# Second block's mixers: all differences of the first row block ahead of the last taps, and the convolution's transposes one quarter unit later

## What is computed

```python
def diff_attention(q, k, v, lam, slopes):
    ...
        s = s - slopes[None, :, None, None, None] * dist
        p = jax.nn.softmax(s, axis=-1)
        a = p[:, :, 0] - lam * p[:, :, 1]
        return jnp.einsum("bhqk,bkhe->bqhe", a.astype(v.dtype), v)

def conformer_conv(u, w_dw, b_dw, ln_g, ln_b):
    a, gate = jnp.split(u, 2, axis=-1)
    z = a * jax.nn.sigmoid(gate)
    z = lax.conv_general_dilated(...) + b_dw        # 31 taps, 256 channels, one filter each
    return jax.nn.silu(layer_norm(z, ln_g, ln_b))

y = jnp.concatenate([y_conv, y_pool, y_attn], axis=-1) @ w_out[l]
```

## Time and profile before

| what | us |
|---|---|
| median of three runs | 2058.48 |
| the profiled execution, whole | 2058.67 |
| its span from the first to the last instruction | 2056.8 |
| TensorE busy in the span | 2043.0 |
| VectorE busy | 1501.4 |
| ScalarE busy | 1094.8 |
| GpSimd busy | 128.9 |

### The profile page before, as it was taken

How to read it: one execution, slowest core, us unless ns; L and a number is a source line. 1 busy time by engine, 2 the same in 40 slices (tenths; PEclk the granted TensorE clock), 3 DMA queues, 4 the chain that set the end, 5 groups by cost and what they waited for, 6 DMA issues and landing times.

```text
span 2056.8 us, 27845 instructions
## 1 busy us (share of the span) xinstructions
PE 2043.0 (99%) x10803; PEld 1743.8 (85%) x10803; DVE 1501.4 (73%) x2262; ACT 1094.8 (53%) x1640; POOL 128.9 (6%) x140
## 2 busy tenths in 40 slices
PE   9999999999999999999999999999999999999998
PEld 8888888888888888888888888878888888878887
DVE  7776677777677767777766777798667777798766
ACT  5444665544554456655446455675445545675443
POOL 1000100000000001000001000160000000160000
PEclk9999999999999999999999999999999999999999
DMA  8655545555555555455555756426555656425553
GB/s 255 201 188 163 195 152 199 185 184 193 191 186 184 194 166 174 167 191 191 187 193 189 240 185 225 154 97 201 191 193 189 205 185 217 161 94 195 194 191 127
DMA packets 105540, 378.82 MB, mean 184 GB/s; under 512 B 12174, under 2 KB 12838, under 8 KB 105153
## 3 DMA queue, kind: packets, MB, share of 16 engines
q1 hardware_dynamic: 102224, 368.16, 54.5%
q0 software_dynamic: 2208, 7.71, 1.2%
q10 hardware_dynamic: 976, 1.17, 0.2%
HBM read 375.73 MB, written 1.27 MB: 183 GB/s over the span
## 4 chain that ended last, share of the span: by engine, by line
PE 95%; DVE 3%; DMA 1%; issue 0%; ACT 0%; SPq 0%; POOLq 0%; POOL 0%; DVEq 0%; ACTq 0%
PE pb L515 30%; PE pb L523 16%; PE pb L414 14%; PE pb L415 14%; PE pb L419 14%; DMA raw<-in_W 1%; PE pb L575 1%; PE pb L442 1%; PE pb L462 1%; PE pb L464 1%; PE pb L463 1%; DVE scr L1821 1%; DVE wlo L1806 1%; DVE scr L2500 0%; PE pb L639 0%
## 5 line engine op out<-in xcount | busy, mean ns | idle before, releaser
L1806 DVE TENSOR_TENSOR wlo<-raw,whi 128x1024 fp32r<-128x1024 f32 (+1 forms) x680 | 822.8, 1218 | 52.4 <-ACT whi L1177 52.2
L1177 ACT ACTIVATE whi<-raw 128x1024 fp32r<-128x1024 f32 (+1 forms) x684 | 707.1, 1045 | 279.1 <-PE pb L523 156.0
L515 PE MATMUL pb<-XT,whi 128*128 128x512 f32 x2784 | 695.2, 391 | 1.3 <-DVE XT L1821 0.7
L515 PEld LDWEIGHTS pb<-XT,whi 128*128 128x128 f32 x2784 | 509.8, 188 | 100.1 <-ACT whi L1177 1.4
L523 PEld LDWEIGHTS pb<-XT,wlo 128*128 128x128 f32 x2784 | 379.7, 190 | 27.1
L523 PE MATMUL pb<-XT,wlo 128*128 128x256 f32 x2784 | 388.2, 282 | 0.0
L1931 DVE TENSOR_REDUCE sbuf_s<-pb 128x256 f32<-128x512 f32 x240 | 154.6, 686 | 230.6 <-PE pb L523 230.6
L414 PE MATMUL pb<-whi,HTh 128*128 128x512 f32 x796 | 313.6, 394 | 0.7 <-DVE HTl L1950 0.4
L415 PE MATMUL pb<-whi,HTl 128*128 128x512 f32 x796 | 311.6, 391 | 0.0
L419 PE MATMUL pb<-wlo,HTh 128*128 128x512 f32 x796 | 302.0, 389 | 0.0
L1248 ACT ACTIVATE sbuf_s<-sbuf_s 128x256 f32<-128x256 f32 x120 | 49.6, 419 | 340.2 <-DVE sbuf_s L1938 340.1
(11 more groups left out here) (267 smaller groups left out, 1663.5 us busy)
## 6 DMA issues: line engine op xcount, KB each, us to landing
raw<-in_W SPq DMA_DIRECT2D x694, 512.0 KB, 4.3
raw<-in_W SPq DMA_DIRECT2D x8, 264.0 KB, 2.8
scr<-in_bc POOLq DMA_DIRECT2D x2, 640.0 KB, 5.3
raw<-in_W SPq DMA_DIRECT2D x4, 256.0 KB, 6.2
scr<-scratch POOLq DMA_DIRECT2D x8, 128.0 KB, 4.5
scr<-mrow POOLq DMA_DIRECT2D x2, 512.0 KB, 5.2
scr<-in_slope POOLq DMA_DIRECT2D x1, 1024.0 KB, 11.2
scr<-in_Pg POOLq DMA_DIRECT2D x1, 1024.0 KB, 14.4
```

The source lines that it names most:

```text
L515: pe.matmul(pb[b + j][:, :], h[:, k:k + P], xs, start=c == 0, stop=False)
L1177: return act.activation(o, i, ACT.Copy, scale=scale)
L1806: dve.tensor_tensor(low_w(u)[:, 0:c], raw[u % RAW_SLOTS][:, 0:c], high_w(u)[:, 0:c].bitcast(F32), ALU.subtract).then_inc(*up("lo", u))
```

## The change

On TensorE the transposes of the convolution, `turn_conv(4)`, go from ahead of the quarter `out(18, 2)` to behind it. On VectorE the four differences of row block 0 go ahead of the taps 26 to 30 and stand in a row; the taps follow, with `pool_low(0, 7)` after tap 28. The three small steps of the weights of row block 1 stand in a row, two of its differences come ahead of the statistics, and the other two between `conv_stats` and `conv_mean`. ScalarE, GpSimd and SyncE keep their order, and no instruction is added or taken away.

```diff
@@ tensor: mixer2 @@
                 out(18, 1)
                 turn_maps(0, 2, 6)
                 turn_maps(0, 0, 5)
+                out(18, 2)
                 turn_conv(4)
-                out(18, 2)
                 values(0, 7)
                 turn_maps(1, 2, 6)
                 turn_maps(1, 0, 5)
@@ vector: mixer2 @@
                 pool_low(1, 7)
+                difference(0, 3)
+                difference(0, 2)
+                difference(0, 1)
+                difference(0, 0)
                 tap(26)
-                difference(0, 1)
                 tap(27)
-                difference(0, 3)
                 tap(28)
+                pool_low(0, 7)
                 tap(29)
-                difference(0, 2)
-                difference(0, 0)
+                tap(30)
                 weights_inv(1)
-                tap(30)
                 weights_ratio(1)
-                pool_low(0, 7)
                 weights_lam(1)
+                difference(1, 2)
+                difference(1, 3)
                 conv_stats(0, 4)
                 conv_stats(1, 4)
+                difference(1, 1)
+                difference(1, 0)
                 conv_mean(0)
                 conv_mean(1)
-                difference(1, 0)
                 conv_var()
-                difference(1, 1)
-                difference(1, 3)
-                difference(1, 2)
                 conv_norm(0, 4)
                 conv_norm(1, 4)
```

## The result

The changed kernel takes 2061.84 us, the median of 20 runs (2060.36 to 2064.15). The kernel before took 2058.45 in 20 runs beside it. The ratio is 1.0016, with a 95% interval of 1.001 to 1.0022, so the change costs 3.4 us (2 to 4.5). That is within the 0.2% that the prediction calls no change, and slower beyond its interval.

What follows compares the result with a forecast made beforehand. TensorE, 95% of the chain, was taken as the bound. Per stage 1.14 us of gaps go and 2.7 come, taken as +1.45; two stages add 2.9 to 2058.48, giving 2061.4 us, range 2059.3 to 2064.0.

Steps and rivals of the forecast that it cites:

- Part 1: First maps: with the four differences first, TensorE's 0.72 us gap falls away; eight transposes run 36.07 to 36.94.
- Part 2: Taps before `turn_conv`: tap 30 ends at 38.10, a new TensorE gap of 0.5 us; `values(0)` ends 0.25 us earlier.
- Part 3: Second maps and statistics: nothing covers GpSimd's root, `conv_norm` ends at 43.4, TensorE waits about 2.0 us before `turn_normed`.
- The sum: One stage loses 1.14 us of gaps and gets 2.7, taken as +1.45 us; two stages +2.9, so 2061.4 us.
- What is queued behind: VectorE's later splits, the weight refill and the tail slide together with TensorE by 1.45 us; costed at nothing.
- B: VectorE's chained steps go at the pace of free ones, root starts 0.5 us sooner: +1.9 us, 2060.4; chance 0.14.
- C: TensorE's gaps go and nothing replaces them: 2.3 us less, 2056.2; chance 0.04.
- D: TensorE's clock falls during the 2 us stall, 1.9 us lost in each stage: 2065.2; chance 0.05.
- E: The weight refill lands late and the tail waits up to 1.95 us more a stage: 2065.3; chance 0.11.

Runs made afterwards that it cites:

- the run that covers the root again: The changed kernel with `conv_mean` and `conv_var` ahead of `difference(1, 1)` and `(1, 0)`; median +1.4 us against the kernel before, ratio 1.0007.
- VectorE's part alone: The kernel before with only the change's new VectorE order, `turn_conv` still ahead of `out(18, 2)` on TensorE; 2061.24 us, ratio 1.0011.
- `turn_normed` later: The changed kernel with `turn_normed` moved behind `out(19, 1)` on TensorE; median +3.0 us against the kernel before, ratio 1.0014.
- the last run: The kernel before with quarter units in TensorE's gaps, maps `(1, 0)` earlier, `turn_normed` behind `out(19, 1)`, VectorE's splits and `conv_low` reordered; 2057.66 us, ratio 0.9996.

## Why the prediction was right, point by point

The time was forecast as 2061.4 us and +2.9; it is 2061.84 and +3.4, by the stages +3.1. By the steps of the prediction, in its count (second stage of the kernel before, subtract 1.85 from the times of the changed trace):

- **Part 1.** The first eight transposes without a gap, from 36.07: measured 1837.92 - 1.85 = 36.07. Two slow differences, the four in 2.7 us: measured 2.71.
- **Part 2.** `turn_conv` at 38.15, measured 38.22. `values(0)` from 38.6, measured 38.71.
- **Part 3.** `difference(1, 2)` at 38.65, measured 38.77; `conv_var` at 41.25, measured 41.37. Each is 0.12 late: the three small steps start 0.23, 0.19 and 0.27 us apart and not 0.2, which is 0.09, and the steps before had summed to 0.03 more (`L2514` at 38.08, forecast 38.05). The root was to take 0.87 us and took 0.71, with VectorE idle beside it; this took the 0.12 back, and `conv_norm` starts at 42.36, forecast 42.4. That it comes out so close is luck: the two errors cancel. The wait for `(1, 0)` does not show as one, but the eight transposes of row block 1 took 1.32 us where 1.03 is their pace.
- **The sum.** `turn_normed` at 43.45, measured 43.50; the matmul behind it at 43.9, measured 43.89. I took 1.45 us a stage, it is 1.48. The stall was to be 2.0 us. It is shown as 1.69, and counted as in the forecast, from where TensorE could have issued (1842.35 + 1.32 - 0.28 + 0.11 = 1843.50), it is 1.85.
- **What is queued behind.** Costed at nothing beyond the slide, and right: 1.51 and 1.56 us at the tail.
- **The rivals.** B, chained steps at the pace of free ones: three chained taps took 1.51 us and two 1.00, two free differences 0.88. It falls. The Trainium skill ("VectorE: DVE Perf Modes", The DRAIN you can't avoid) measured eight `tensor_copy` with a semaphore behind each and behind the last alone, and found no difference. No run here takes a semaphore away; what the rows show for these scaled sums is that one that needs the one before costs 0.1 us more than a free one. So I had stretched that figure too far when I took it for rival B. C, the gaps go and nothing replaces them: the gaps went, and the root with `conv_norm` took their place. D, the clock: the changed stage ran at 1.00 through its stall of 1.69 us, so the stall did not bring the clock down in this execution. The fall that one later run shows has another place. It also gives the price with a granted clock beside it, 2.08 us against 1.13. The rows from the start that the prediction priced D by take double the time too, but the view shows a granted clock of 1.00 for that stretch, so that they stand at the level of 1.2 GHz is read from their pace alone. E, the refill: 6.31 us, as before.

The first explanation of the 1.48 us as the root alone would have been too simple. The prediction's sum held it together with the chained steps, but my expectation for the run that covers the root again gave 1.0 us of it to the cover alone, and missed by 0.45 us.

What stays open: in most of the experiments that were slower than before, the median lies 0.4 to 0.9 us under the sum of the stages (one agrees), while for the change itself it lies 0.3 over. All of that is inside the intervals. For the two profiled executions of the main comparison the 0.3 has a place: the first stage begins at 1370.99 us before and at 1371.33 in the changed kernel, ahead of every edit. Over the ten profiled executions here that place lies between 1369.88 and 1371.83, with different waits of TensorE before it, so differences of 1 us and more can come from there whatever the stages do. The clock has a part in the spread too. In 20 runs of the changed kernel the mean granted clock was 1.0 in five, with a median of 2061.06, and 0.998 in seven, with 2062.45; of the 75 runs of the kernel before beside the experiments 8 had 0.998, and of the 22 of the two experiments with VectorE's new order unaltered (VectorE's part alone, `turn_normed` later) 2. Whether the changed kernel meets the lower clock more often I can't tell.

## What to carry to other kernels

When one engine works through a fixed list and another takes its results at several places, time gained at the first of them was worth nothing here, because the whole list was not sooner. Look for the last result that is waited for and what stands in front of it. A short round trip to another engine (here a root of 0.7 us) needs independent work placed between its question and its answer, and dependent steps alternated with independent ones took less of VectorE's time here (0.40 against 0.69 us for the three small ones). If the gap is on the engine that waits, it can be filled there with its own work that needs nothing: that gave 0.39 us up to `values(1)`, read from the stages and not confirmed by the medians.

## What the hardware did that I had not expected

- GpSimd's root of 128x2 took 0.71 us with VectorE idle, 0.87 beside differences and 1.61 beside a split; that of 128x4 took 1.91 beside a split and, in the last run, 1.01 where VectorE stood idle for the first 0.68 of it:

```profile
1846.17 1.01 POOL L2790 TENSOR_TENSOR st<-st,cst 128x4 f32<-128x4 f32 x1 [4.55 <-DVE st L1832]
```

- TensorE's granted clock fell to the level of 1.2 GHz for some 3 us in one execution, behind small matmuls with waits of at most 0.88 us between them, and that cost 1.5 us. In the kernel before it stayed at 2.4 GHz behind the same matmuls and waits, and in the changed one through a wait of 1.69 us between larger matmuls.
